# A two-layer hybrid decoder with 64 experts a layer: two more weight buffers, and half of a shared product moved behind the first expert

## The reference, cut to what matters

```
h = concat(meta(16 x 1024), x(256 x 1024))              # T = 272 tokens
for i in range(2):                                      # two layers
    mix = rwkv7_time_mix(h) if i == 0 else swa_sink_attention(h)
    h = layer_norm(ALPHA * h + mix)
    scores = sigmoid(h @ router)                        # 64 experts
    idx = top 8 of 64, from the best 4 of 8 groups      # per token
    gate = scores[idx] / sum * 2.5
    routed = sum over the 8 of gate * swiglu(h, w_gate[e], w_up[e], w_down[e])   # 1024 -> 256 -> 1024
    shared = swiglu(h, shared_w_gate, shared_w_up, shared_w_down)                # the same widths, all tokens
    h = layer_norm(ALPHA * h + shared + routed)
return h[16:]
```

## Time and profile before

| | us |
|---|---|
| median of 3 runs | 1621.53 (1621.11 to 1623.51) |
| the profiled execution, its own time | 1621.35 |
| its span, from the first to the last instruction | 1619.6 |
| TensorE busy | 1449.4 (89% of the span) |
| DVE busy | 614.1 (38%) |
| POOL busy, ACT busy | 327.4, 318.4 (20% each) |
| moved by DMA | 508.42 MB |

### The profile page before, as it was taken

The page is one execution under the profiler, slowest core; times in us unless marked ns, Lnnn a source line. Parts: engine busy times, 40 slices in busy tenths (PEclk is TensorE's granted clock), DMA queues, the critical chain, the costliest instruction groups (busy, mean ns, idle before and its releaser), DMA issues.

```text
span 1619.6 us, 33331 instructions
## 1 busy us (share of the span) xinstructions
PE 1449.4 (89%) x12804; PEld 937.7 (58%) x12804; DVE 614.1 (38%) x1580; ACT 318.4 (20%) x743; POOL 327.4 (20%) x404
## 2 busy tenths in 40 slices
PE   6989988799999998888886699999999998888884
PEld 4777878647556655555553267575566655555541
DVE  5352343654333333333322704453333333223326
ACT  2531333111111111111111016211111111111110
POOL 6012000011222222222222030022222222222210
PEclk9999989799999999999999799999999999999998
DMA  6340002496999999999997995469999999999986
GB/s 203 113 130 1 3 4 81 163 360 255 394 413 413 414 415 416 415 415 415 415 415 301 374 321 183 159 232 395 412 412 414 415 415 415 416 415 416 415 339 254
DMA packets 139878, 508.42 MB, mean 314 GB/s; under 512 B 29273, under 2 KB 58273, under 8 KB 104188
## 3 DMA queue, kind: packets, MB, share of 16 engines
q1 hardware_dynamic: 103312, 456.49, 70.9%
q0 software_dynamic: 22288, 41.89, 7.3%
q10 hardware_dynamic: 14172, 8.54, 1.9%
HBM read 501.38 MB, written 36.90 MB: 332 GB/s over the span
## 4 chain that ended last, share of the span: by engine, by line
PE 55%; SPq 27%; DMA 8%; DVE 6%; issue 3%; ACT 1%; POOL 0%; POOLq 0%; DVEq 0%
SPq L836 27%; PE ps L784 13%; PE ps L802 7%; PE ps L1466 6%; DMA arena<-in_moe_w_up 5%; PE ps L1596 3%; PE ps L765 3%; PE ps L772 2%; PE ps L1019 2%; PE ps L1898 2%; PE ps L2000 2%; DMA ring<-in_moe_w_up 2%; PE ps L1029 1%; PE ps L791 1%; DMA arena<-routed 1%
## 5 line engine op out<-in xcount | busy, mean ns | idle before, releaser
L784 PE MATMUL ps<-arena 128*64 128x256 f32 x2752 | 314.4, 381 | 54.2 <-DMA arena<-in_moe_w_up 42.7
L784 PEld LDWEIGHTS ps<-arena 128*64 128x64 f32 x2752 | 211.1, 137 | 187.1 <-issue 117.0
L777 DVE COPY arena<-ps 128x512 f32<-128x512 f32 x128 | 88.5, 692 | 448.9 <-PE ps L772 448.9
L821 POOL DMA_INDIRECT arena<-hrows,arena x128 | 130.3, 1018 | 548.4 <-DVE arena L817 532.7
L784 PE MATMUL ps<-ring,arena 128*64 128x256 f32 x1344 | 153.5, 381 | 23.6 <-DMA ring<-in_moe_w_up 22.0
L826 POOL DMA_INDIRECT routed<-arena x128 | 117.0, 914 | 246.6 <-DVE arena L952 226.7
L802 PE MATMUL ps<-arena 128*64 128x512 f32 x688 | 166.6, 605 | 0.0
L952 DVE TENSOR_SCALAR arena<-ps,arena 64x512 f32<-64x512 f32 x128 | 95.1, 743 | 167.8 <-PE ps L802 167.8
L784 PEld LDWEIGHTS ps<-ring,arena 128*64 128x64 f32 x1344 | 99.8, 137 | 90.9 <-issue 37.2
L906 ACT COPY arena<-ps 128x256 f32<-128x256 f32 x128 | 47.6, 372 | 495.7 <-PE ps L784 495.7
L916 ACT ACTIVATE arena<-ps,arena 64x512 f32<-64x512 f32 x128 | 87.5, 683 | 208.2 <-PE ps L802 208.2
(11 more groups left out here) (360 smaller groups left out, 1533.0 us busy)
## 6 DMA issues: line engine op xcount, KB each, us to landing
arena<-in_moe_w_down SPq DMA_DIRECT2D x86, 1024.0 KB, 24.2
arena<-in_moe_w_gate SPq DMA_DIRECT2D x86, 1024.0 KB, 24.5
arena<-in_moe_w_up SPq DMA_DIRECT2D x86, 1024.0 KB, 24.4
ring<-in_moe_w_gate SPq DMA_DIRECT2D x42, 1024.0 KB, 24.5
ring<-in_moe_w_up SPq DMA_DIRECT2D x42, 1024.0 KB, 24.3
ring<-in_moe_w_down SPq DMA_DIRECT2D x42, 1024.0 KB, 24.1
arena<-routed SPq DMA_DIRECT2D x16, 1024.0 KB, 14.6
ring<-in_attn_w_qkv SPq DMA_DIRECT2D x6, 1024.0 KB, 16.4
```

The lines of the kernel that those rows point to most:

```text
L777: return nc.vector.tensor_copy(xgT.rearrange("p (r j) m -> p j r m", r=2), ps[:, bU, :].rearrange("p (j r m) -> p j r m", j=4, r=2))
L784: mm = nc.tensor.matmul(dst[SLOTS * j:SLOTS * j + SLOTS, 0:FF], xgT[:, k, :], slots[pair[j]][:, FF * k:FF * k + FF], start=(k == 0), stop= ...
L821: return nc.gpsimd.indirect_dma_start(out=dst, out_offset=None, in_=hrows_d[l], in_offset=bass.IndirectOffsetOnAxis(ap=index, axis=0), bou ...
```

## The change

Seven edits, in both layers:

1. The arena grows from 33864 to 36936 floats a partition, and two more slots are made (`FIRST`): one over the router's work space (free from step "sel"), one in the new room. The room comes from the descriptor scratch of POOL's DMAs, set to 4096 bytes a partition.
2. Expert 0 reads its gate and up from the two `FIRST` slots. Places 0 and 1 take gate and up of expert 6 from the start.
3. SP's order: up of expert 0 first of all; the loads of places 0 and 1 (now of expert 6) go behind the others; then gate of expert 0, which waits for "sel" and for the stored rows, then places 15, 16, 17. Expert 6's gate and up fall out of the later order.
4. The counts are done in five wider products, not nine.
5. `su1` moves from before expert 0 to behind its first part (gate and up, and the transposes), in another bank, and waits for the first shared product on DVE ("sm0").
6. The pick of expert 1 goes behind expert 0's first transposes, that of expert 2 behind expert 0's gate and up; the indexes on DVE follow.
7. The two "sd" steps of the last 16 tokens become one, of eight products of 256 columns in four column groups, and the steps stand behind experts 1 to 5.

```diff
-ARENA = 33864
+ARENA = 36936
...
+FIRST = (3 * SETS, 3 * SETS + 1)
...
+            slot_free[FIRST[0]] = moe_dve[l].at("sel")
+            slot_free[FIRST[1]] = (main.gu, 1) if l else None
...
+            + [view(6272, SLOT), view(33864, SLOT)]
...
         def e_slots(e):
             k = 3 * (e[1] % SETS)
+            if early(e, 0):
+                return FIRST + ORDER[2:3]
             return ORDER[k:k + 3]
...
         def sp_enter(sp, L, l, *places):
             for i in places:
+                e = (0, SETS if i < 2 else i // 3)
                 if L.entry_free[ORDER[i]]:
                     sp.wait_ge(*L.entry_free[ORDER[i]])
-                sp_fetch(sp, l, (0, i // 3), i % 3)
+                sp_fetch(sp, l, e, i % 3)
+        def sp_first(sp, L, l, j):
+            if L.entry_free[FIRST[j]]:
+                sp.wait_ge(*L.entry_free[FIRST[j]])
+            if j == 0:
+                sp.wait_ge(rows_stored, 16 * 3 * (l + 1))
+            sp_fetch(sp, l, (0, 0), j)
...
                 mm_gate_up(ps[:, bG, :], (s0, s1)).then_inc(L.gu, 1)
+                if early(e, 0):
+                    pe_pick(pe, L, (0, 2))
...
-        DOWN_TURNS = (1, 2, 3, 5, 6, 7)
+        DOWN_TURNS = (1, 2, 3, 4, 5)
...
+                for q in range(4 if u == 4 else 0):
+                    m = nc.tensor.matmul(ps[32 * q:32 * q + n, bS[0], 0:256], shm[:, j, r0:r0 + n],
+                                         shared_w[2][:, D * j + 256 * q:][:, 0:256], start=(j == 0), stop=(j == 1))
...
             mm_shared(pe, l, "su0", range(2, KC))
-            pe_pick(pe, L, (0, 1))
-            mm_shared(pe, l, "su1", range(KC // 2))
-            pe_pick(pe, L, (0, 2))
-            mm_shared(pe, l, "su1", range(KC // 2, KC))
             pe.wait_ge(*moe_act[l].at("sg1"))
             pe_turn_x(pe, L, l, (0, 0))
+            pe_pick(pe, L, (0, 1))
             def body(e):
                 pe_expert(pe, L, l, e)
+                if early(e, 0):
+                    pe.wait_ge(*moe_dve[l].at("sm0"))
+                    mm_shared(pe, l, "su1", range(KC))
...
-                    sp_enter(sp, main, l, *range(11))
+                    sp_first(sp, main, l, 1)
+                    sp_enter(sp, main, l, *range(2, 11))
                     shared(l, 0, rv.at("res0_2"))
                     sp_enter(sp, main, l, 11, 12)
                     shared(l, 1, rp.at("o1_1"))
-                    sp_enter(sp, main, l, 13, 14)
+                    sp_enter(sp, main, l, 13, 14, 0, 1)
...
+                sp_first(sp, main, l, 0)
                 sp_enter(sp, main, l, 15, 16, 17)
                 sp_experts(sp, main, l)
...
-                for t in range(NT + 1):
-                    for t2 in range(min(t + 1, NT)):
-                        k2 = TILES[t2][1]
-                        m = mm_(ps[:, bC, E * t:E * t + E], (before if t2 == t else allones)[0:k2, :], sel[0:k2, t2, :],
-                                start=(t2 == 0), stop=(t2 == min(t, NT - 1)))
+                few_rows = TILES[-1][1]
+                for t2 in range(NT - 1):
+                    mm_(ps[:, bC, E * (t2 + 1):NT * E + E].rearrange("p (t e) -> p t e", e=E), allones[:, :],
+                        sel[:, t2, :].unsqueeze(1).to_broadcast([P, NT - t2, E]), start=(t2 == 0), stop=False)
...
-    nc = _bacc.Bacc("TRN2", target_bir_lowering=False, num_devices=1)
+    nc = _bacc.Bacc("TRN2", target_bir_lowering=False, num_devices=1, dynamic_dma_scratch_size=4096)
```

More of the change, by code:

```diff
@@ L281, in hybrid_trunk @@
         moe_pe = [Steps(sem(f"route_pe{l}"), [(f"hT{t}", 1 if t == 2 else 2) for t in H_ORDER[l]]
-                        + [("lg", 1), ("sT", 1), ("sg0", 1), ("sg1", 1), ("pos", 1), ("su0", 1), ("su1", 1), ("sd", 6)])
+                        + [("lg", 1), ("sT", 1), ("sg0", 1), ("sg1", 1), ("pos", 1), ("su0", 1), ("su1", 1), ("sd", 5)])
                   for l in range(2)]
@@ L289, in hybrid_trunk @@
                             ("kr", 1), ("dest", 3), ("posm", 1), ("sm0", 1), ("max", 1), ("maxi", 1), ("sm1", 1),
-                            ("sd", 6)]) for l in range(2)]
+                            ("sd", 5)]) for l in range(2)]
         ON_PE, ON_DVE_FIRST, ON_DVE_LAST = (0, 1, 3, 5), (2, 4), (6, 7)
@@ L444, in plan_experts @@
                 slot_free[slot] = moe_pe[l].at("su1")
-            main_slots.append((list(slot_count), list(slot_free)))
+            slot_free[FIRST[0]] = moe_dve[l].at("sel")
+            slot_free[FIRST[1]] = (main.gu, 1) if l else None
+            count = list(slot_count)
+            for slot in ORDER[0:2]:
+                count[slot] -= 16
+            main_slots.append((count, list(slot_free)))
             done = (l + 1) * E
+            for slot in FIRST:
+                slot_count[slot] += 16
             for i, slot in enumerate(ORDER):
-                slot_count[slot] += 16 * len(range(i // 3, E, SETS))
+                slot_count[slot] += 16 * (len(range(i // 3, E, SETS)) - (i < 2))
                 slot_free[slot] = (main.down if i % 3 == 2 else main.gu, done)
@@ L666, in hybrid_trunk @@
         slots = [ring[:, i, :] for i in range(RING)] + [view(8704 + SLOT * i, SLOT) for i in range(5)] \
-            + [view(21760 + SLOT * i, SLOT) for i in range(4)] + [view(SLOT * i, SLOT) for i in range(3)]
+            + [view(21760 + SLOT * i, SLOT) for i in range(4)] + [view(SLOT * i, SLOT) for i in range(3)] \
+            + [view(6272, SLOT), view(33864, SLOT)]
         shared_w = [slots[15], slots[16], lnrow[:, :, :].rearrange("p a b -> p (a b)")]
@@ L937, in dve_expert @@
                 dve_mark(dve, L, plus(e, 3))
+            if this and early(e, 0):
+                dve_index(dve, L, (0, 2))
             if this and ahead(e, 1):
@@ L996, in turn @@
             def turn(e):
-                if not isinstance(e[0], int) or e[1] >= SETS:
+                if not isinstance(e[0], int) or e[1] > SETS:
                     sp_load(sp, L, l, e, (0, 1))
@@ L1074, in dve_shared_down @@
             dve.wait_ge(*moe_pe[l].at("sd", u))
+            if u == 4:
+                for q in range(4):
+                    cs = slice(256 * q, 256 * q + 256)
+                    add = nc.vector.scalar_tensor_tensor(out=h[0:n, 2, cs], in0=h[0:n, 2, cs], scalar=ALPHA,
+                                                         in1=ps[32 * q:32 * q + n, bS[0], 0:256], op0=ALU.mult, op1=ALU.add)
+                add.then_inc(*moe_dve[l].step("sd", u))
+                return
             nc.vector.scalar_tensor_tensor(out=h[0:n, u // 2, cs], in0=h[0:n, u // 2, cs], scalar=ALPHA,
```

25 lines of the change are left out of this document (16 added, 9 removed).

## The result

The changed kernel is slower: 1628.7 us median of 11 runs (1625.3 to 1636.6) against 1621.53 (11 runs too, 1616.3 to 1624.5 but for one of 6039.7), ratio 1.004 with an interval of 1.0021 to 1.0059. The profiled execution took 1626.54 us, 5.2 more than that of before, for a span of 1624.8.

A forecast was written before the change was run, and what follows sets the result against it. It took each layer to be bound, from 384 us on, by an unbroken load stream at the DMA rate, 2.75 us a load; 7.9 - 5.5 = +2.4 us a layer, 1621.4 + 4.8 = 1626.2 us, range 1618.5 to 1630.

The forecast's parts named there:

- The sum: Per layer: stream start 7.9 us later, less 5.5 us for two loads fewer, +2.4; +4.8 for both layers.
- The counts gain nothing, the gather goes out as before, TensorE idles until it lands: Before expert 0: wider counts gain at most 0.05 us; gather issued at 376.84, landing 3.2 us later; TensorE idle from 378.45.
- rival 1: Expert 0's first gather is slowed by running loads and lands after 7.1 us: +6.0 us a layer, 1633; chance 0.12.
- The stream starts 7.9 us later: Place 16, waiting for shared up now behind expert 0, goes out at 391.8 and not at 383.86 in layer 0.
- Two loads fewer gain 5.5 us; a late start costs what it is late: Weight stream: 18 loads issued ahead instead of 16 save 2 x 2.75 us a layer; the 7.9 us late start counts fully.
- From 384 on the queue is never empty: Weight loads in layer 0: those issued between 390 and 450 us need 10.1 us to land, more than three times 2.75.
- rival 2: The weight stream follows TensorE's slot releases, not the DMA rate: -1.6 us a layer, 1618.2; chance 0.17.
- The grouped shared down is hidden: Last 16 tokens' shared down: 0.9 us for two steps of 1.98, 3.1 us of TensorE less, hidden by later load waits.

The follow-up runs named there:

- e4: The changed kernel with a dummy product in each of TensorE's two idle stretches before expert 0; ratio to before 1.0039.
- e7: The changed kernel with the shared down steps behind experts 56 to 60 and the next layer norm's rows loaded behind expert 61; ratio to before 0.9997.
- e1: The changed kernel with shared up and the picks put back before expert 0, the two buffers kept; ratio to before 1.0006.
- e3: The kernel before with only the five wider counts, the grouped shared down and the smaller descriptor scratch; ratio to before 1.0010.
- e2: The changed kernel without the two buffers, SP's order as before, shared up still behind expert 0; ratio to before 1.0057.
- e6: e1 with the shared down behind experts 56 to 60 and the layer norm's rows loaded behind expert 61; ratio to before 0.9963.
- e5: e3 with the shared down behind experts 56 to 60 and the layer norm's rows loaded behind expert 61; ratio to before 0.9971.
- e9: e7 with a dummy product in each of TensorE's two idle stretches before expert 0; ratio to before 0.9999.
- e10: e6 with the nine counts of the kernel before in place of the five wider ones; ratio to before 0.9989.
- e8: The changed kernel with both halves of shared up before expert 0's transposes and e5's shared down and layer norm placement; ratio to before 1.0009.

## Why the prediction was right, and where its terms were not

The sum said +2.4 us a layer and 1626.2 in all; the traces show +3.9 and +1.3, the profiled execution took 1626.5, and the ratio's 6.5 us lie within the range. That the sum came so near is in part luck: without the half clock, which is not in the sum, a layer lost 1.3 and 1.4 us (e4) and not 2.4, and both terms of the sum were worth less than they were put at. By steps:

- **The counts gain nothing, the gather goes out as before, TensorE idles until it lands.** Right. The idle stretch was 1.49 us (forecast 1.55), the transposes came 3.1 us after the gather's issue (3.2). The first gather was an unloaded one in both layers (2.97 and 2.98 us), so rival 1 fell. In e7, layer 0, it took longer, 4.4 us; why, no run shows.
- **The stream starts 7.9 us later.** Place 16 went out 7.4 us later in layer 1 and, filled, in e4 (7.4 in both layers): right to 0.5 us. In layer 0 it was 9.2, and the excess over layer 1 is the half clock, of which the prediction spoke nowhere.
- **Two loads fewer gain 5.5 us; a late start costs what it is late.** As a sum the two came near: 7.4 - 5.5 = 1.9, and in layer 1 of the changed kernel the 20th load landed 0.6 us, the 60th 1.4 and the last 1.3 us later after the first gather than before. As terms they were mis-sized, since they are not independent. The two loads without the late start are worth little (e1 against e3: 0.6 us worse in layer 0, 1.2 better in layer 1); beside a start that is equally late (16.2), 1.7 us (changed against e2, layer 0). The late start alone cost 5.4 of 9.1 us (e2).
- **The step behind this that failed** is "From 384 on the queue is never empty: a load issued between 390 and 450 us needs 10.1 us to land, more than three times 2.75". The 10.1 is the number of the second load of a burst of three, and an idle queue already needs 4.7 us for one. The gates are the ones to read: 7.1 us before, so the queue was about one load deep when a release came, 5.6 with two loads more in front (e1), 12.7 where releases are quick (e6). Up to expert 8 the stream was limited in part by releases, which came every 9 us behind the first experts, where three loads need 8.25. It wasn't dry, so rival 2's faster time didn't come; but its mechanism was there in part, for the queue was thin enough that an earlier start was mostly waited away, and a later one partly made up.
- **The grouped shared down is hidden.** It took 1.06 us (forecast 0.9), and e3 shows nothing of it. But the place of the shared down behind the first experts is not free, as the prediction had it: with it in the tail the last product came 3.1 to 5.0 us a layer sooner where no half clock stood in the way (e5 against e3 in layer 1, e6 against e1, e9 against e4). The layer norm's rows moved with it, and no run moves one without the other; but their 1 MB has passed by the end of the layer in both. I missed it by reading the queue as deep.
- **The rest of the time** moves from execution to execution. At 60 to 70 us, long ahead of the change, the granted clock was 0.66 in the profiled execution of before and 1.00 in that of the changed kernel, which is most of the 3.4 us by which its first gather was early; at 905 to 915 us it was 1.00 and 0.83, and layer 1's first gather came 3.5 us later behind layer 0's last load. These rows are before's and then the changed kernel's, each 60 to 70 us:

```profile
60.00:70.00 10.00, 10.00 (x30) 6.27 (x30) 8.47 (x18) 3.98 (x9) 0.53 (x1) 0.66 0.29 71
```

```profile
60.00:70.00 10.00, 10.00 (x102) 7.05 (x102) 9.16 (x21) 6.50 (x13) 0.53 (x1) 1.00 0.50 139
```

That these stretches have nothing to do with the change was not tried by itself; but half clock there comes and goes in kernels with the two buffers (e1 and e10 without it, e4 and e6 with it) and in kernels without them (e5 without it, e3 with it).

What stays open: the price of the change within 0.2 to 0.6%. And e6, 0.6% better than the changed kernel by the last loads of its two layers and 0.4% better than before by its ratio, is not told from e10 by either.

## What to carry to other kernels

Before a load stream is called limited by bandwidth, read the landing time of the first load behind each release, and take off what one load needs in an idle queue: 4.7 us of the 7.1 were no queue at all. Buffers that only let loads start earlier gain what the releases behind them can keep up, so look first at what delays the early releases; here two lines that moved the shared down (and the layer norm's rows) to where TensorE waits anyway gave what two more megabytes alone did not. And an operation that fills a wait (shared up, while the first gather flew) is not free to move, even when nothing in the chain of dependences holds it there.

## What the runs showed of the hardware that was not expected

Short idle stretches of TensorE were followed by half clock. In the six layers of the profiled executions with the two stretches before expert 0 (0.9 and 1.5 to 2.9 us; changed, e2, e7), the granted clock fell to half there in five, for 3.4 to 6.8 us; in e8, with the longer stretch one expert later, in both layers. With the first of the stretches alone ahead of expert 0 (0.87 us; e1, e3, e5, e6, e8) it fell in two of ten, and in none of the eight with neither or with both filled by a dummy product (before, e4, e9, e10). The price was 1.7 us on gate and up, 5.36 against 3.67. Not every short stretch was: the dummy products left 0.4 to 0.9 us of idle time before the transposes, without half clock behind it, and the 0.78 us before expert 0's gate and up, in both layers of before, e1, e3, e5, e6 and e10, was not followed by half clock in any of these twelve layers. That the idle stretches are the cause rests on these counts and on e4 and e9, where about 2 us of dummy products took it away.
